# A feed-forward part split into two phases, with both matrix products by Strassen's scheme

## The chip, the core and the metric

The kernel runs on one core of a Trainium2 chip. The metric is the device time of one launch in microseconds (us). TensorE (PE in the profile) multiplies matrices into PSUM, which has eight banks of 128 x 512 floats; VectorE (DVE) and ScalarE (ACT) read and write PSUM and SBUF, GpSimd (POOL) reads and writes SBUF alone, and SyncE (SP) issues the DMAs. Each engine works through its own instructions in order and waits on semaphores.

## The reference

One layer of a streaming encoder trunk is computed for 1024 prompt tokens and 64 sample tokens. The change touches its last lines, the feed-forward part:

```python
D_MODEL = 1024; D_FF = 4 * D_MODEL          # tokens: 1024 + 64
x = x + rms_norm(merged @ lp['w_out'], lp['post_mix_gain'])
u = jax.nn.relu(rms_norm(x, lp['pre_ffn_gain']) @ lp['w_up'])      # 1024 -> 4096
return x + rms_norm((u * u) @ lp['w_down'], lp['post_ffn_gain'])   # 4096 -> 1024
```

## The kernel before

All large products are made in "fp32 parts": an operand x is held as a rounded part hi (ScalarE's copy) and a remainder lo = x - hi (a subtraction on GpSimd or VectorE), both in a type that TensorE takes at full rate, and a product is three matmuls, hi*hi, hi*lo and lo*hi (`three_products`, L315 to L321). The 64 sample tokens are partly multiplied in plain fp32 instead (`product_apart`, L324), in two halves of 64 rows.

`block_out` (L2363) makes the output projection, the residual and the norm, and leaves the normed tokens transposed in f_hi and f_lo (128 x 8 x 1152). It already issues the first four units of the up projection (`up_unit`), and turns the last token group last, so the fifth unit starts at 1569.0 us of the trace.

`block_ffn` (L2587) then goes over eight groups of 512 hidden features. In a group, 12 *up units* (`FF_UPS`: four blocks of 128 features by token groups of 384, 384 and 320) fill a PSUM bank each with 24 matmuls; ScalarE takes relu and square, VectorE the square's remainder, and so u_hi and u_lo for this group stay in SBUF. Then 16 *down units* (two halves of 512 output columns by eight tiles of 128 tokens, 12 matmuls each) and two fp32 products for the sample tokens give partial results, which VectorE adds into the accumulator `big` (L2756). Weights come in four slabs of 1 MB per group through a ring of two places: SP loads, ScalarE rounds (L2695), GpSimd subtracts (L2664). The loop over groups is a hardware loop, and TensorE waits for a slab's split, a bank's release and the squares' remainders. After the last group each tile is squared and summed (ScalarE), multiplied by the gain and given its inverse root (GpSimd), normed and added to x2 (VectorE, `last_norm`), and stored.

Of the kernel before, what the change touches and what calls it, by code (L numbers as in the profile page):

```python
# [126 lines left out]
def build(nc, io):  # L127
    with ExitStack() as ctx:
# [3 lines left out]
        g.sem = lambda name: ctx.enter_context(nc.semaphore(name))  # L132
# [12 lines left out]
        g.d_x2 = dram("d_x2", (T_ALL, D_MODEL))  # L145

# [5 lines left out]
        weight_ring(g)  # L152
        with ExitStack() as first:
# [26 lines left out]
        with ExitStack() as last:  # L180
            g.big = last.enter_context(nc.sbuf_tensor("big", [P, N_TILE * D_MODEL], F32))
# [42 lines left out]
            g.h_at = -(-nc.sbuf_base // 64) * 64  # L224
            g.h_hi = last.enter_context(nc.sbuf_tensor("f_hi", [P, KT, T_PAD], F32R))
            g.h_lo = last.enter_context(nc.sbuf_tensor("f_lo", [P, KT, T_PAD], F32R))
            out = block_out(g)
            ffn = block_ffn(g, out)
            with nc.Block() as block:
                @block.sync  # L230
                def _(sp):
                    out.on_sync(sp)
                    ffn.on_sync(sp)

                @block.tensor
                def _(pe):
                    out.on_tensor(pe)
                    ffn.on_tensor(pe)

                @block.scalar  # L240
                def _(act):
                    out.on_scalar(act)
                    ffn.on_scalar(act)

                @block.gpsimd
                def _(pool):
                    out.on_gpsimd(pool)
                    ffn.on_gpsimd(pool)

                @block.vector  # L250
                def _(dve):
                    out.on_vector(dve)
                    ffn.on_vector(dve)
# [2103 lines left out]
FF_G = 512  # L2357
FK = FF_G // P
FF_UPS = [(f + e, c0, n) for f in range(0, FK, 2) for c0, n in GROUPS for e in range(2)]
# [3 lines left out]
def block_out(g):  # L2363
# [17 lines left out]
    with ExitStack() as ctx:  # L2381
# [22 lines left out]
        stage.up_full, stage.normed = up_full, n2  # L2404
        stage.x2_stored = [(x2_out[j], out_before[j] + 16 * len(range(j, N_TILE, NX))) for j in range(NX)]
# [181 lines left out]
def block_ffn(g, out):  # L2587
    nc, io = g.nc, g.io
    n0 = g.slab
    N_GRP = D_FF // FF_G  # L2590
    g.slab += 4 * N_GRP
    assert n0 % 2 == 0
    w_up, w_down = io["w_up"][0], io["w_down"][0]
    acc = g.big[:].rearrange("p (i c) -> p i c", c=D_MODEL)
    ups = FF_UPS
    downs = [(half, i) for half in range(2) for i in range(N_TILE)]
    NU, ND = len(ups), len(downs)
    B_UP, B_DN = 4, 3
    up_full = out.up_full
    LEAD = 4  # L2600
    with ExitStack() as ctx:
        sb = lambda name, shape, dt=F32: ctx.enter_context(nc.sbuf_tensor("ff_" + name, shape, dt))
        u_hi, u_lo = sb("u_hi", [P, FK, T_PAD], F32R), sb("u_lo", [P, FK, T_PAD], F32R)
        both, u_late = sb("relu_sq", [P, 4, 384]), sb("u_late", [P, FK, DEC])
        relu, sq = both[:, 0:2, :], both[:, 2:4, :]
        ss, expo = sb("ss", [P, N_TILE, 2]), sb("expo", [P, 1])

        x2 = nc.alloc_sbuf_tensor_at("ff_x2", [P, N_TILE, D_MODEL], F32, offset=g.h_at)
        gain = nc.alloc_sbuf_tensor_at("ff_gain", [P, D_MODEL], F32, offset=g.h_at + 4 * N_TILE * D_MODEL)
        junk = both[:].rearrange("p a b -> p (a b)")[:, 0:D_MODEL]  # L2610
        outs = [io["y_prompt"][0, i * P:(i + 1) * P, :] for i in range(TILE_P)] + [io["y_sample"][0]]
        sem = lambda name: g.sem("ff_" + name)
        gain_in, y_squared, roots, normed, y_done, y_out = (sem(n) for n in (
            "gain_in", "y_squared", "roots", "normed", "y_done", "y_out"))
        unfolded, gained = sem("unfolded"), sem("gained")
        (up_free, squared, sq_made, u_ready, dn_full, acc_done) = (sem(n) for n in (
            "up_free", "squared", "sq_made", "u_ready", "dn_full", "acc_done"))

        stage = Stage()
        @stage.sync  # L2620
        def _(sp):
            def load(i, s):

                n, slot = n0 + 4 * i + s, s % 2
                if s < 2:
                    sp.wait_ge(dn_full, i * ND - ND + N_TILE * (s + 1))
                else:
                    sp.wait_ge(g.w_split, n - 1)
                if s < 2:
                    src = w_up[:, bass.ds(i * FF_G + s * 256, 256)].rearrange("(k p) c -> p k c", p=P)  # L2630
                    k = KT
                else:
                    src = w_down[bass.ds(i * FF_G, FF_G), (s - 2) * 512:(s - 1) * 512].rearrange(
                        "(k p) c -> p k c", p=P)
                    k = FK
                sp.dma_start(g.w_raw[:, slot, :].rearrange("p (k c) -> p k c", k=k), src
                             ).then_inc(g.w_loaded[slot], 16)


            with sp.Fori(0, N_GRP - 1) as i:  # L2640
                load(i, 2)
                load(i, 3)
                load(i + 1, 0)
                load(i + 1, 1)
            load(N_GRP - 1, 2)
# [11 lines left out]
        def _(pool):  # L2657
# [10 lines left out]
            with pool.Fori(0, N_GRP - 1) as i:  # L2668
                for s in range(1, 5):
                    split(n0 + 4 * i + s, s % 2)  # L2670
# [200 lines left out]
```

## Time and profile before

| | us |
|---|---|
| median of 3 runs (lowest to highest) | 2325.13 (2324.92 to 2329.96) |
| span of the profiled execution | 2324.8 |
| TensorE busy in the span | 2262.7 (97%) |
| VectorE, ScalarE, GpSimd busy | 1219.2 (52%), 712.7 (31%), 658.6 (28%) |

The profiled execution's own time is its span, 2324.8 us, 0.3 under the median; the trace shows nothing of what lies around it. Busy times of TensorE overlap, as its matmuls are pipelined, so distances between starts are read in place of durations. "Granted clock" is the share of 2.4 GHz that TensorE had.

### The profile page before, as it was taken

To read this page: it belongs to the slowest core of one execution; us is meant where nothing else is said; L and a number is where in the kernel's file an instruction comes from. 1 tells how busy PE (TensorE), PEld (TensorE's weight loads), DVE (VectorE), ACT (ScalarE), POOL (GpSimd) and SP (SyncE) were. 2 spreads that over 40 slices of the span, in tenths; PEclk is the share of its full clock that TensorE was granted. 3 is DMA by queue.
4 is the path that set the end of the run, shared out by engine and by line. 5 is a ranking of instruction groups with operands and counts; after the bars stand their busy time and mean duration, and the time that the engine had idled before them with its cause. 6 is when DMAs were issued, how large, how long until landed. Compare 5 with 4: busy or idle time off the path is not lost. (4 is left out here: it accounts for less than half of the span.)

```text
span 2324.8 us, 40590 instructions
## 1 busy us (share of the span) xinstructions
PE 2262.7 (97%) x16447; PEld 2107.6 (91%) x16447; DVE 1219.2 (52%) x2113; ACT 712.7 (31%) x1483; POOL 658.6 (28%) x742
## 2 busy tenths in 40 slices
PE   7999999999999999999999999999999999999998
PEld 6998999999999889878889999988989889898896
DVE  4125699999992677255543655164323333243335
ACT  5234421212121244455544423252212122121122
POOL 3453631212322788200001221152212112121215
PEclk9999999999999999999999999999999999999999
DMA  5351222323233644532116533140201201112014
GB/s 171 112 139 55 66 85 82 103 81 100 88 101 119 184 137 114 162 111 73 57 45 216 177 122 114 40 145 21 71 19 54 72 18 54 33 40 72 18 54 163
DMA packets 207209, 214.39 MB, mean 92 GB/s; under 512 B 30521, under 2 KB 188433, under 8 KB 207057
## 3 DMA queue, kind: packets, MB, share of 16 engines
q1 hardware_dynamic: 207056, 212.27, 29.1%
q8 instruction: 106, 1.74, 0.3%
q14 instruction: 47, 0.38, 0.1%
HBM read 152.80 MB, written 59.43 MB: 91 GB/s over the span
## 5 line engine op out<-in xcount | busy, mean ns | idle before, releaser
L306 POOL TENSOR_TENSOR w_lo<-w_raw,w_hi 128x2048 fp32r<-128x2048 f32 (+2 forms) x41 | 174.0, 4244 | 593.5 <-ACT w_hi L299 593.5
L2664 POOL TENSOR_TENSOR w_lo<-w_raw,w_hi 128x2048 fp32r<-128x2048 f32 x31 | 143.0, 4613 | 578.6 <-ACT w_hi L2695 578.6
L319 PE MATMUL ps<-f_hi,w_hi 128*128 128x384 f32 (+1 forms) x768 | 251.3, 327 | 1.6 <-ACT ff_relu_sq L2704 1.6
L319 PE MATMUL ps<-h_hi,w_lo 128*128 128x384 f32 (+1 forms) x768 | 250.5, 326 | 0.0
L319 PE MATMUL ps<-h_lo,w_hi 128*128 128x384 f32 (+1 forms) x768 | 250.3, 326 | 0.0
L319 PE MATMUL ps<-f_hi,w_lo 128*128 128x384 f32 (+1 forms) x768 | 250.3, 326 | 0.0
L319 PE MATMUL ps<-h_hi,w_hi 128*128 128x384 f32 (+1 forms) x768 | 250.3, 326 | 0.0
L319 PE MATMUL ps<-f_lo,w_hi 128*128 128x384 f32 (+1 forms) x768 | 250.1, 326 | 0.0
L748 ACT ACTIVATE p_stage<-ps 128x256 f32<-128x256 f32 (+5 forms) x203 | 83.8, 415 | 519.0 <-PE ps L319 519.0
L2756 DVE TENSOR_TENSOR big<-big,ps 128x512 f32<-128x512 f32 x144 | 94.8, 658 | 262.3 <-PE ps L319 244.2
L2743 DVE TENSOR_TENSOR ff_relu_sq<-ff_relu_sq 128x384 f32<-128x384 f32 (+1 forms) x96 | 102.6, 1069 | 208.8 <-ACT ff_relu_sq L2704 208.6
L319 PE MATMUL ps<-w_hi,h_hi 128*128 128x256 f32 x712 | 204.6, 287 | 3.6 <-DVE h_lo L438 3.6
L319 PE MATMUL ps<-w_lo,h_hi 128*128 128x256 f32 x712 | 202.8, 285 | 0.0
L319 PE MATMUL ps<-w_hi,h_lo 128*128 128x256 f32 x712 | 202.7, 285 | 0.0
L319 PE MATMUL ps<-w_hi,ff_u_hi 128*128 128x512 f32 x512 | 200.1, 391 | 0.0
L319 PE MATMUL ps<-w_lo,ff_u_hi 128*128 128x512 f32 x512 | 199.3, 389 | 0.0
L319 PE MATMUL ps<-w_hi,ff_u_lo 128*128 128x512 f32 x512 | 199.2, 389 | 0.0
L1076 DVE MAX8 ix_m<-ix_work 128x8 f32<-128x1024 f32 (+6 forms) x191 | 168.2, 881 | 6.6
L2695 ACT ACTIVATE w_hi<-w_raw 128x2048 fp32r<-128x2048 f32 x31 | 59.2, 1909 | 341.2 <-DMA w_raw<-in_w_up 341.2
L1078 DVE MATCH_REPLACE8 ix_work<-ix_m,ix_work 128x1024 f32<-128x1024 f32 (+6 forms) x184 | 159.0, 864 | 0.0
L319 PEld LDWEIGHTS ps<-f_hi,w_hi 128*128 128x128 f32 x768 | 144.1, 188 | 4.7 <-issue 4.5
L319 PEld LDWEIGHTS ps<-f_lo,w_hi 128*128 128x128 f32 x768 | 144.2, 188 | 0.0
(239 smaller groups left out, 5407.7 us busy)
## 6 DMA issues: line engine op xcount, KB each, us to landing
w_raw<-in_w_in SPq DMA_DIRECT2D x34, 1024.0 KB, 5.5
w_raw<-in_w_up SPq DMA_DIRECT2D x16, 1024.0 KB, 5.6
w_raw<-in_w_down SPq DMA_DIRECT2D x16, 1024.0 KB, 5.2
gm_gate<-d_gate SPq DMA_DIRECT2D x48, 192.0 KB, 2.6
d_gate<-gatef_stage SPq DMA_DIRECT2D x28, 192.0 KB, 2.5
gm_y_raw<-d_y SPq DMA_DIRECT2D x8, 576.0 KB, 5.0
n_x<-in_x_prompt SPq DMA_DIRECT2D x8, 512.0 KB, 9.1
w_raw<-in_w_mem_kv SPq DMA_DIRECT2D x4, 1024.0 KB, 6.3
```

The lines of the kernel that those rows point to most:

```text
L306: engine.tensor_tensor(g.w_lo[:, s, 0:size], g.w_raw[:, s, 0:size], g.w_hi[:, s, 0:size].bitcast(F32), ALU.subtract).then_inc(g.w_split, 1)
L319: last = pe.matmul(out, left(a, kk), right(b, kk), start=(kk == 0 and n == 0), stop=(kk == k - 1 and n == 2))
L748: nc.scalar.activation(stage[0:r, n % NS, 0:c], g.ps[0:r, n % NB, 0:c], sl.func).then_inc(staged, 1)
L1076: link(v.max(m8, sc if it == 0 else left))
L1078: link(v.match_replace(left, m8, sc if it == 0 else left, NEG))
L2664: G.tensor_tensor(g.w_lo[:, slot, :], g.w_raw[:, slot, :], g.w_hi[:, slot, :].bitcast(F32), ALU.subtract).then_inc(g.w_split, 1)
L2695: S.activation(g.w_hi[:, slot, :], g.w_raw[:, slot, :], ACT.Copy).then_inc(g.w_rounded, 1)
L2743: V.tensor_tensor(sq[:, u % 2, 0:n], relu[:, u % 2, 0:n], relu[:, u % 2, 0:n], ALU.mult).then_inc(sq_made, 1)
L2756: V.tensor_tensor(dst, dst, g.ps[:, 4 + d % B_DN, 0:n], ALU.add).then_inc(acc_done, 1)
```

## The change

The feed-forward part becomes two blocks, `block_up` and `block_down`, with all activations u stored to a DRAM tensor d_u (4096 x 1088) between them. Both are products of 2 x 2 blocks and use seven block products in place of eight (Strassen's scheme in Winograd's form), with the sums and differences of blocks made on VectorE.

**Up.** Features go in 16 chunks of 256. The first two are made as before ("plain", eight units beside the four of `block_out`); meanwhile VectorE, GpSimd and ScalarE make the three sums and differences of token blocks (S1, S2, S4, and S3 in the place of a quarter of f_hi and f_lo) with hi and lo parts, each 128 x 2048. The other 14 chunks are seven products of 12 matmuls of 512 columns each. For each chunk four differences of weight blocks (128 x 512) are made on VectorE, seven operands are rounded on ScalarE and subtracted on GpSimd, five PSUM sums (`combine`) and three relu-squares are made on VectorE, and the 64 sample tokens are one fp32 product and one transposition.

**Down.** Four groups of 1024 features. In a group the blocks are 512 tokens by 512 features and 512 features by 512 outputs, seven products of 48 matmuls. Operands have two places each; a product's operands are rounded on ScalarE once the product two before is done, and subtracted on GpSimd (tokens) and VectorE (weights). VectorE makes eight sums of blocks in each group (`make`), keeps 28 PSUM tiles (`keep`), and in the last group GpSimd adds the seven accumulators together (`fold`, five of 128 x 2048, the last two after the operands of products 2 and 3) before the final norm. Two pieces are hung into the last chunk of the up block: the loads of the first two blocks (`early`), and the first weight remainder (`first_lo`), which stands on VectorE ahead of that chunk's last sum.

```diff
-FF_G = 512
-FF_UPS = [(f + e, c0, n) for f in range(0, FK, 2) for c0, n in GROUPS for e in range(2)]
+FF_UPS = [(e, c0, n) for c0, n in GROUPS for e in range(2)]
...
             with nc.Block() as block:
                 def _(sp):
+                    for fresh in up.fresh + down.fresh:
+                        sp.sem_clear(fresh)
                     out.on_sync(sp)
-                    ffn.on_sync(sp)
+                    up.on_sync(sp)
+                    down.on_sync(sp)
...
-def block_ffn(g, out):
+CH, PLAIN = 256, 2
+PARTS = [("11", "X"), ("S1", "Z"), ("S2", "Y"), ("12", "X"), ("S3", "Y"), ("S4", "Z"), ("22", "Y")]
+def block_up(g, out):
...
+    def _(pool):
+        split_slab(g, pool, n0 + 1, SLAB)
+        pool.wait_ge(late_made, 1)
+        G.tensor_tensor(v_c[:], hi.bitcast(F32), low.bitcast(F32), ALU.add).then_inc(raw11, 1)
+        pool.wait_ge(s_hi, 1)
+        G.tensor_tensor(sums["S1"][1][:], v_b[:], sums["S1"][0][:].bitcast(F32), ALU.subtract).then_inc(s_lo_pool, 1)
+        pool.wait_ge(s_hi, 3)
+        G.tensor_tensor(sums["S4"][1][:], v_b[:], sums["S4"][0][:].bitcast(F32), ALU.subtract).then_inc(s_lo_pool, 1)
...
+    def _(act):
+        for u in range(4):
+            relu_plain(u)
+        round_sum(sums["S1"][0][:], v_b[:], 3)
+        relu_plain(4)
+        round_sum(sums["S2"][0][:], v_c[:], 5)
+        relu_plain(5)
+        round_sum(sums["S4"][0][:], v_b[:], 7)
+        hi(PLAIN, 0)
+        relu_plain(6)
...
+    def _(pe):
+        for u in range(UP_EARLY, len(plain)):
+            pe.wait_ge(freed, u - 3)
...
+                if p == 0 and c + 1 < N_CH:
+                    late(c + 1)
+                if p == 3 and c + 1 < N_CH:
+                    turn_late(c + 1)
...
+    def _(dve):
+        square_plain(0)
+        whole(v_a[:], a21)
+        square_plain(1)
+        whole(v_b[:], h_of["22"])
+        square_plain(2)
+        dve.wait_ge(summed, 2)
+        V.tensor_tensor(v_b[:], v_a[:], v_b[:], ALU.add).then_inc(summed, 1)
+        square_plain(3)
+        dve.wait_ge(raw11, 1)
+        V.tensor_tensor(v_a[:], v_c[:], v_a[:], ALU.subtract).then_inc(summed, 1)
+        dve.wait_ge(summed, 3)
+        V.tensor_tensor(v_c[:], v_b[:], v_c[:], ALU.subtract).then_inc(summed, 1)
+        square_plain(4)
+        dve.wait_ge(s_hi, 2)
+        V.tensor_tensor(sums["S2"][1][:], v_c[:], sums["S2"][0][:].bitcast(F32), ALU.subtract).then_inc(s_lo_dve, 1)
+        dve.wait_ge(s_lo_pool, 1)
+        whole(v_b[:], h_of["12"])
+        square_plain(5)
+        dve.wait_ge(summed, 6)
+        V.tensor_tensor(v_b[:], v_b[:], v_c[:], ALU.subtract).then_inc(summed, 1)
+        t_first(PLAIN)
+        square_plain(6)
...
+        square_plain(8)
+        t_second(PLAIN)
...
+        for c in chunks:
+            for j, bank, other, p in ((1, y_bank, v, 4), (2, z_bank, u, 5), (3, y_bank, first, 6)):
+                if j == 3 and c == N_CH - 1:
+                    stage.before_last_sum(dve)
+                combine(made(j), bank, other, [(prod, q_of(c, p) + 1), (combined, n + j + 1)])
+                relu_square(c, j)
...
+def block_down(g, up):
+    def early(sp):
+        load_b(sp, 0, "11")
+        stored(sp, 3)
+        load_a(sp, 0, "11")
...
+    def _(sp):
+        stored(sp, N_CH - 1)
+        sp.wait_ge(up.prod, up.q_of(N_CH - 1, 5) + 1)
+        load_a(sp, 0, "12")
+        load_b(sp, 0, "21")
+        load_b(sp, 0, "12")
+        load_b(sp, 0, "22")
+        sp.dma_start(u_late[:], g.d_u[0:2 * HALF, SEQ:T_ALL].rearrange("(k p) t -> p k t", p=P)).then_inc(l_in, 16)
+        load_a(sp, 0, "21")
+        load_a(sp, 0, "22")
...
+    def _(pool):
+        lo(0, 0)
+        for i in range(N_DG):
+            for p in range(7):
+                if i == LAST and p == 0:
+                    pool.wait_ge(kept, 28 * LAST)
+                    fold(Y2, Z1)
+                    fold(Y1, Z2)
+                if 7 * i + p + 1 < 7 * N_DG:
+                    lo((7 * i + p + 1) // 7, (p + 1) % 7)
+                if i == LAST and p == 0:
+                    pool.wait_ge(kept, 28 * LAST + 4)
+                    pool.wait_ge(folded, 1)
+                    fold(Y2, X1)
...
+    def _(pe):
+            for p, (name, chain) in enumerate(D_PARTS):
+                if p == 2:
+                    late(i, 4 * (chain_no % 2) + 3)
+                pe.wait_ge(a_lo, q + 1)
+                pe.wait_ge(b_lo, q + 1)
...
+        def make(i, j):
+            if j == 0:
+                dve.wait_ge(a_in["21"], 16 * (i + 1))
+                dve.wait_ge(a_in["22"], 16 * (i + 1))
...
+        MAKE_AFTER = {(0, 0): 0, (0, 1): 1, (1, 0): 2, (1, 1): 3, (1, 3): 4, (2, 0): 5, (2, 2): 6, (2, 3): 7}
+        SPLIT_AFTER = {0: 2, 1: 2, 2: 1, 3: 1, 4: 1, 5: 1, 6: 1}
+        normed_at = {(5, 0): 1, (5, 2): 1, (5, 3): 1, (6, 0): 1, (6, 1): 1, (6, 2): 1, (6, 3): 3}
+        for i in range(N_DG):
+            for p in range(7):
+                for t in range(4):
+                    keep(i, p, t)
+                    if (p, t) in MAKE_AFTER:
+                        make(i, MAKE_AFTER[p, t])
+                    if (p, t) == (1, 3):
+                        keep_late(i)
+                    if SPLIT_AFTER[p] == t:
+                        split_next(i, p)
+                    if i < LAST:
+                        continue
+                    if (p, t) == (3, 0):
+                        unfold()
+                    if (p, t) == (5, 0):
+                        dve.wait_ge(gain_in, 16)
+                    for _ in range(normed_at.get((p, t), 0)):
+                        last_norm(n_normed)
+                        n_normed += 1
```

## Rows read from the trace of the kernel before

**Rows 1.** Busy time, share of the span and instructions of each engine.
```profile
PE 2262.7 (97%) x16447; PEld 2107.6 (91%) x16447; DVE 1219.2 (52%) x2113; ACT 712.7 (31%) x1483; POOL 658.6 (28%) x742
```
**Rows 2.** Busy time by stretch (us, engines, clock, DMA): whole feed-forward, one group.
```profile
1569.00:2315.10 746.10, 744.47 (x4002) 666.39 (x4000) 269.88 (x401) 158.99 (x253) 164.08 (x62) 1.00 0.15 52
1623.59:1718.69 95.10, 95.10 (x514) 85.38 (x513) 31.69 (x46) 19.08 (x28) 18.45 (x4) 1.00 0.14 45
```
**Rows 3.** Chain of waits in order of time (start, us, what): one down phase.
```profile
2124.90 69.36 PE ps L319 x384
```
**Rows 4.** Timeline of ACT (start, us): relu at the end of three up units.
```profile
1590.71 0.49 ACT L2704 ACTIVATE ff_relu_sq<-ps 128x384 f32<-128x384 f32 x1 [3.11 <-PE ps L319]
...
1594.87 0.49 ACT L2704 ACTIVATE ff_relu_sq<-ps 128x384 f32<-128x384 f32 x1 [3.11 <-PE ps L319]
...
1598.39 0.44 ACT L2704 ACTIVATE ff_relu_sq<-ps 128x320 f32<-128x320 f32 x1 [2.46 <-PE ps L319]
```
**Rows 5.** Timelines of DVE and POOL: two down units' additions beside a subtraction.
```profile
1604.66 0.69 DVE L2756 TENSOR_TENSOR big<-big,ps 128x512 f32<-128x512 f32 x1 [1.16 <-PE ps L319]
1607.38 0.69 DVE L2756 TENSOR_TENSOR big<-big,ps 128x512 f32<-128x512 f32 x1 [2.03 <-PE ps L319]
...
1604.73 4.61 POOL L2664 TENSOR_TENSOR w_lo<-w_raw,w_hi 128x2048 fp32r<-128x2048 f32 x1 [16.80 <-ACT w_hi L2695]
```
**Rows 6.** Timeline of PE: one fp32 product of the sample tokens, earlier projection.
```profile
158.18 1.97 PE L328 MATMUL ps<-w_raw,h_late 128*64 128x128 f32 x32
```
**Rows 7.** Timelines of DVE and POOL: a square beside a subtraction.
```profile
1583.63 4.71 DVE L2743 TENSOR_TENSOR ff_relu_sq<-ff_relu_sq 128x384 f32<-128x384 f32 x1 [1.19 <-ACT ff_relu_sq L2704]
1588.38 0.56 DVE L2749 TENSOR_TENSOR ff_u_lo<-ff_relu_sq,ff_u_hi 128x384 fp32r<-128x384 f32 x1
...
1583.31 4.62 POOL L2664 TENSOR_TENSOR w_lo<-w_raw,w_hi 128x2048 fp32r<-128x2048 f32 x1 [11.32 <-ACT w_hi L2695]
```
**Rows 8.** Timelines of DVE and POOL: one VectorE product, three GpSimd subtractions in a row.
```profile
1031.96 0.82 DVE L2101 TENSOR_SCALAR at_prob<-at_prob,at_den 128x384 f32<-128x384 f32 x1
...
1030.07 3.84 POOL L1172 TENSOR_TENSOR w_lo<-w_raw,w_hi 128x512 fp32r<-128x512 f32 x3
```
**Rows 9.** Groups of instructions of DVE, by form (busy us, mean ns).
```profile
L306 DVE TENSOR_TENSOR w_lo<-w_raw,w_hi 128x2048 fp32r<-128x2048 f32 x7 | 16.0, 2291 | 61.7 <-ACT w_hi L299 61.7
...
L2764 DVE SCALAR_TENSOR_TENSOR big<-big,ff_ss,ff_gain 128x512 f32<-128x512 f32 x8 | 6.0, 751 | 0.1
```
**Rows 10.** Groups of instructions of POOL, by form, from 1450 us on.
```profile
L2664 POOL TENSOR_TENSOR w_lo<-w_raw,w_hi 128x2048 fp32r<-128x2048 f32 x31 | 143.0, 4613 | 578.6 <-ACT w_hi L2695 578.6
...
L2677 POOL TENSOR_TENSOR big<-big,ff_gain 128x512 f32<-128x512 f32 x8 | 10.2, 1287 | 7.0 <-ACT ff_relu_sq L2726 7.0
...
L2681 POOL TENSOR_TENSOR ff_ss<-ff_ss 128x1 f32<-128x1 f32 x8 | 4.5, 566 | 8.1 <-ACT ff_relu_sq L2726 8.1
```
**Rows 11.** Groups of instructions of ACT, by form, from 1450 us on.
```profile
L2695 ACT ACTIVATE w_hi<-w_raw 128x2048 fp32r<-128x2048 f32 x31 | 59.2, 1909 | 341.2 <-DMA w_raw<-in_w_up 341.2
```
**Rows 12.** Timeline of POOL: the first subtraction of the feed-forward stage.
```profile
1567.36 4.64 POOL L2664 TENSOR_TENSOR w_lo<-w_raw,w_hi 128x2048 fp32r<-128x2048 f32 x1 [13.92 <-ACT w_hi L2695]
```
**Rows 13.** DMA issues by line (KB each, median us to landing).
```profile
w_raw<-in_w_down SPq DMA_DIRECT2D x16, 1024.0 KB, 5.2
...
out_y_prompt<-big SPq DMA_DIRECT2D x8, 512.0 KB, 2.6
```
**Rows 14.** Busy time by stretch: two 1 MB loads at once, ten 256 to 512 KB loads (last: GB/s).
```profile
2271.00:2281.00 10.00, 10.00 (x45) 8.29 (x45) 2.11 (x4) 2.90 (x8) 8.76 (x5) 1.00 1.02 415
1652.00:1657.00 5.00, 5.00 (x31) 5.00 (x30) 0.00 (x0) 1.78 (x1) 0.00 (x0) 1.00 1.04 365
```
**Rows 15.** Who PE waited for (us in total, times, longest).
```profile
PE ps L319 <- DVE f_lo L2563: 3.8, 1, 3.8
...
PE ps L319 <- ACT ff_relu_sq L2704: 1.6, 1, 1.6
```
**Rows 16.** Busy time by stretch, right after the 3.8 us wait (clock third from the end).
```profile
1429.42:1432.83 3.41, 2.88 (x13) 2.91 (x14) 3.41 (x4) 3.41 (x5) 0.00 (x0) 0.50 0.97 284
```

More of the change, by code:

```diff
@@ L247, in _ @@
                     out.on_gpsimd(pool)
-                    ffn.on_gpsimd(pool)
+                    up.on_gpsimd(pool)
+                    down.on_gpsimd(pool)
                 @block.vector
@@ new lines, in block_up @@
+    g.slab += N_CH
+    at = lambda name, shape, offset, dt=F32: nc.alloc_sbuf_tensor_at("up_" + name, shape, dt, offset=offset)
+    KB = 1024
+    q1, q2 = g.big_at, g.rest_at
+    work = [at(f"work{j}", [P, KH, HALF], q1 + 8 * KB * j) for j in range(3)]
+    v_b, v_c, v_a = work
+    sq = at("sq", [P, 4, 384], q1 + 24 * KB)
+    h_late = at("h_late", [P, KT, DEC], q1 + 30 * KB)
+    lt, lu = at("lt", [P, 2, P], q1 + 32 * KB), at("lu", [P, 2, P], q1 + 33 * KB)
+    t3 = at("t3", [P, KH, P], q1 + 34 * KB)
@@ new lines, in block_up @@
+    late_full, late_kept, late_sq, late_turned, late_out = (sem(n) for n in (
+        "late_full", "late_kept", "late_sq", "late_turned", "late_out"))
+    st_out = [sem(f"st_out{j}") for j in range(NST)]
+    lu_out = [sem("lu_out0"), sem("lu_out1")]
+    plain = [(c, e, c0, n) for c in range(PLAIN) for e, c0, n in FF_UPS]
+    q_of = lambda c, p: 7 * (c - PLAIN) + p
+    chunks = range(PLAIN, N_CH)
+    raw = lambda c: g.w_raw[:, c % 2, :].rearrange("p (k f) -> p k f", k=KT)
+    B = lambda c, a, b: raw(c)[:, a * KH:(a + 1) * KH, b * P:(b + 1) * P]
@@ new lines, in block_up, with u_stored @@
+    stage.before_last_store, stage.before_last_sum = None, None
+    stage.last_evicted = [(combined, 5 * len(chunks)), (x_kept, len(chunks)), (late_kept, len(chunks)),
+                          (late_out, len(chunks))]
+    def u_stored(c):
+        counts = [(sq_out[j], 16 * len([u for u in range(len(plain)) if u % 4 == j and plain[u][0] <= c]))
+                  for j in range(4)]
+        made = [out_index(d, j) for d in chunks if d <= c for j in range(4)]
+        counts += [(st_out[j], 16 * len([e for e in made if e % NST == j])) for j in range(NST)]
+        lates = [d for d in chunks if d <= c]
+        counts += [(lu_out[j], 32 * len([d for d in lates if d % 2 == j])) for j in range(2)]
+        return [(s, n) for s, n in counts if n]
```

841 lines of the change are left out of this document (633 added, 208 removed).

## The prediction

> **What bounds the kernel now.** I read the busy line first: TensorE is busy 97% of the span, the others at most half of it [rows 1]. The view by stretch says the same of the feed-forward part alone: from the fifth up unit at 1569.0 to the last product at 2315.1 TensorE works 744.47 of 746.10 us at full clock [rows 2], and the chain of waits runs through whole down phases without another engine in it [rows 3]. So this part is worth its matmuls; what shortens them shortens the kernel as long as the other engines keep up. They have room now: in a group of 95.10 us VectorE has 31.69 and GpSimd 18.45 busy [rows 2].
>
> Prices of matmuls come from distances. A 384-column unit ends 4.16 us after the one before, a 320-column unit 3.52 [rows 4]; a down unit of 12 matmuls of 512 columns takes 2.72 (two additions apart, [rows 5]), or 0.2267 each. A group holds 8 x 4.16 + 4 x 3.52 + 16 x 2.72 = 90.9; the 4.2 left of 95.1 are two fp32 products of the sample tokens, 2.1 each.
>
> The view that matters for the change is the timelines of VectorE and GpSimd laid side by side. A square with both inputs in SBUF that meets a GpSimd subtraction lasts 4.71 us in place of some 0.55 and ends 0.4 after it [rows 7]; the additions with one input in PSUM keep their 0.69 beside the same subtraction [rows 5]. With three subtractions in a row, a VectorE product of SBUF data got in between them (it ended at 1032.78, the run at 1033.91, [rows 8]). I take it that the two engines exclude each other where VectorE reads SBUF alone, and take turns. Before, there are 31 such subtractions, 143 us in all [rows 10], and VectorE's delays land in slack. The change puts far more on both.
>
> **The change, part by part.** *Matmuls, from 1569.0.* Eight plain units: 4 x 4.16 + 4 x 3.52 = 30.7. Up: 14 chunks x 84 x 0.2267 = 266.6. For the sample tokens 14 fp32 products, 1.97 and some 0.1 for the switch, taken as 2.1 [rows 6], and 14 transpositions, no row, bounded by 0.2 and 0.8 (a tenth and two fifths of such a product), taken as 0.4: 35.0. Down: 4 x 28 x 2.72 = 304.6, and four fp32 products of four times the size of those in [rows 2], 4 x 7.1 = 28.4 (bounds 6.8 and 8.4 each). Together 665.3 against 746.1: 80.8 us less.
>
> *Steady chunks, 21.5 us each.* GpSimd has eight operations of 128 x 512 at 1.29 [rows 10] and a small one, about 10.8; VectorE four differences of 0.69, three relu-squares of 0.75 [rows 9], five sums of 0.69, 8.5. The exclusive part is 10.8 + 5.0 = 15.8 of 21.5. The tightest step is the seventh product, which waits for the sum after the fifth; VectorE has it 0.8 after that product ends, 1.9 before it is due. Loads, stores (six small ones a chunk on SP) and rounding (seven of about 0.6 on ScalarE) are a chunk ahead. Cost nothing; cover is the 5.7 us per chunk.
>
> *The plain part.* Here VectorE makes eight sums and remainders of 128 x 2048 (2.29, [rows 9]) until S4 is ready, GpSimd its slab and v_c at 4.6, S1's and S4's remainders and small ones [rows 10], all excluding each other. GpSimd starts at 1567.4 [rows 12]. In turns: slab to 1572.0, square, v_c to 1577.0, then VectorE: sum, square, sum, square, S1 ready 1584.9. ScalarE stands at S1's rounding (1.91, [rows 11]) with the relu of unit 4 behind it: done 1587.4. Unit 8 needs that bank, due 1584.3: 3.2 late. S2 waits for a GpSimd remainder (1587.8 to 1592.4): 1594.7, rounded 1596.6, relu of unit 5 at 1597.1: unit 9, due 1593.7, 3.5 late. S4 (1604.0) holds the relu of unit 6: unit 10, due 1601.4, 5.7 late. Then the relu of unit 9 stands behind the third weight operand, which waits for t_second behind three squares that take turns with GpSimd (1615.6): the first product starts at 1618.5 instead of 1614.6. Sum 16.3.
>
> *Between the phases*, E being the end of the last up product. GpSimd subtracts the first token operand (4.6) from E-5.6, so the first relu-square of the last chunk waits to E-1.0; behind it two sums, two relu-squares and first_lo: the last sum is done at E+4.2, where the down block starts (4.3 lost), the last relu-square at E+5.0, its store lands at about E+7.1 (2.6 for twice the size, [rows 13]). SP waits for that store, and behind it stand six 1 MB loads and the sample tokens' (0.26 MB): 6.55 MB at 365 GB/s [rows 14] are 17.9, and 2.6 before the first byte (5.2 for a lone load [rows 13] less its 2.9): all landed at E+27.7. After the first tile VectorE stands in make 0, which needs the last two of these loads. Behind it: make 1, two keeps, and the weight remainder of product 1, which also lets a token subtraction pass: done E+39.9. Product 1 was due at E+15.2: 24.7 lost. Bounds: 21 (415 GB/s and no subtraction between) and 38 (each load 5.2 after the other).
>
> The Trainium skill, SBUF — State Buffer, section "A bandwidth-pool intuition that's wrong (but worth ruling out)", puts the HBM's side of a core at about 358 GB/s. The loads of rows 14 were above it, at 365 and 415; by the skill's figure the sum would be 0.4 us higher.
>
> *A later down group*, S being its start. GpSimd subtracts to S+6.5, so make 0, asked for at 3.4, ends at 8.8; keep, make 1, keep to 12.5, weight remainder to 14.8. Product 1, due at 10.9, starts 3.9 late. Where the fifth operand meets make 7 in product 3, 1.6 more. Groups 1 and 2: 11.0. The fp32 product (7.1) before product 2 hides the rest.
>
> *The last group* has five folds of 4.6 on GpSimd, two of them ahead of the operand of product 1. Taking turns: fold to 5.3, make 0 to 7.6, fold to 12.2, make 1 to 14.5, operand to 19.1, weight remainder to 21.4: 10.5 late. The next fold and operand go on to 31.3 with makes between: product 2 starts 3.3 late, product 3 2.7, product 4 12.3 (makes 6 and 7, the last fold and two operands are still queued, then unfold and the weight remainder). In product 5 VectorE reaches the first norm at 3.4 but GpSimd has its operand (to 6.5), five gain products of 1.29 and three root steps of about 0.55 [rows 10]: 14.8. The norm takes 2.2, and only then comes the weight remainder of product 6, done at 20.5 against 10.9 due: 9.6 (bounds 6 and 12). Sum 38.4 (bounds 25 and 50).
>
> *The end.* Before, 9.7 from the last product to the end [rows 2]. After, three norms of 2.2 stand on VectorE behind the last tile and then a store: 13.6, 3.9 more.
>
> *Clock.* A 3.8 us wait was followed by 3.41 us at half clock, a loss of 1.7; a 1.6 us wait was not [rows 15, 16]. The waits above make some twelve candidates: 0 to 20; several fall where TensorE waits again anyway, so 8.
>
> SP clears the new semaphores at the block's start, behind no data that is due soon: 0, at most 5.
>
> Sum: -80.8 + 16.3 + 29.0 + 11.0 + 38.4 + 3.9 + 8 = +25.8 on the execution's 2324.8, 2350.6; with the 0.3 to the median, 2351.
>
> **The rivals.**
> *A, the engines pass each other.* If GpSimd's and VectorE's large operations run side by side, and the 4.71 is something of that one line, the plain part loses nothing, the boundary 22 (the loads stay), later groups 0.8 each, the last 3.6 + 9; the clock 6, the end 3.9: -80.8 + 46 = -35, 2290. For it: VectorE's additions pass [rows 5]. Against it: that form reads PSUM, and the delay ends with GpSimd's instruction to 0.4 us [rows 7]. It decides from the point where a remainder of 2.29 stays 2.29 beside a subtraction.
> *B, the waits outside the loads are a third shorter* (55 of 82), because queues slip apart after the first meeting, as each delay of TensorE gives the others time: -80.8 + 55 + 24.7 = -1, 2324. For it: the walk takes every meeting as it comes. Against it: in the plain part and the last group the exclusive work alone (about 48 us from 1567.4, and some 70 in 51 us of products) is more than the time there is.
> *C, the chunks are bound by preparation*: if meetings add 2 us to each of 14 chunks, 2379. For it: seven GpSimd operations a chunk to meet. Against it: the cover of 5.7.
> *D, the products don't shrink*, as a 512-column matmul in the new order takes longer than 0.2267: at 0.24 the 2520 new ones take 34 us more, 2385. Against it: the same form ran at 0.2267 in 16 units of each group.
>
> **How the numbers follow.** The forecast (waits as walked, 2351, own range 2332 to 2375 from the bounds above) gets 0.63; A, and what lies between it and B on the faster side, 0.18; B around no change 0.13; C and D 0.06. A measurement here can't tell a change under 0.3% (7 us) from none. Faster by more 0.19, within 0.13, slower 0.68. The range 2304 to 2376 leaves out the far end of A and C and D.
>
> **What would show it.** In the changed kernel's trace: TensorE from the first Strassen product about 21.5 per chunk without waits; a TensorE wait of 20 to 30 us at the start of the down block, behind VectorE in make 0, which waits for DMA; VectorE remainders of 128 x 2048 with means well over 2.29 beside GpSimd's 4.6; waits before product 1 of each down group, about 4, and 10 in the last; TensorE busy under 95%. I am wrong if VectorE's large operations keep 2.29 in the down phase, if the first loads land before the store of the last chunk, or if chunks take over 23 us.

## The result: 2344 us, 0.8% slower, and the profile after

The changed kernel takes 2344.09 us (2340.34 to 2345.27) where the one before takes 2325.03 beside it: a ratio of 1.0077, 95% interval 1.0063 to 1.0092. The forecast was 2351, slower. The profiled execution spans 2341.4 us against 2324.8, 16.6 more. Of its time 2.1 us lie outside the span; the kernel before, in the executions beside the experiments, has 1.8 there (2325.37 for a span of 2323.6), so the 0.3 that stands ahead of the prediction was too little, by under 2 us.

The busy line of the page: fewer matmuls than in [rows 1] and less TensorE time, GpSimd 205 us busier and VectorE 188.

```profile
PE 2201.6 (94%) x15877; PEld 1999.9 (85%) x15877; DVE 1407.4 (60%) x2093; ACT 761.8 (33%) x1487; POOL 863.2 (37%) x874
```

Busy time by stretch, in the columns of [rows 2] (products are counted from 0 in each group): plain units, the 14 chunks, down group 0, group 1, the last group, and what stands behind the last product.

```profile
1571.00:1617.90 46.90, 38.08 (x234) 36.72 (x233) 42.26 (x22) 11.75 (x19) 26.57 (x9) 0.93 0.18 59
1617.90:1914.05 296.15, 296.15 (x1605) 242.53 (x1603) 140.60 (x164) 84.13 (x152) 149.41 (x124) 1.00 0.31 102
1914.05:2028.05 114.00, 88.04 (x401) 70.66 (x402) 62.00 (x48) 26.25 (x14) 33.67 (x7) 0.88 0.41 141
2028.05:2117.00 88.95, 85.33 (x402) 68.59 (x401) 57.60 (x44) 26.03 (x14) 34.60 (x7) 0.98 0.29 98
...
2206.00:2328.20 122.20, 90.94 (x400) 71.49 (x399) 94.76 (x61) 33.88 (x44) 86.77 (x37) 0.87 0.16 56
2328.20:2341.40 13.20, 0.01 (x1) 0.00 (x0) 9.49 (x15) 1.45 (x4) 6.94 (x11) 0.58 0.54 199
```

The chunks run without a gap, 21.15 us each. All that is lost is lost around them: TensorE's waits from the fifth up unit on (us in total, times, longest) are 73.3 us, where [rows 2] had under 2.

```profile
PE ps L3322 <- issue: 60.8, 8, 22.3
PE ps L336 <- ACT up_sq L2795: 7.0, 2, 5.0
PE ps L3322 <- DVE up_stage_u L2981: 3.7, 1, 3.7
PE ps L2893 <- POOL up_lt L2756: 1.8, 1, 1.8
```

Line 3322 is the down product. "Issue" there means that the view names no releaser; the timelines do. They place the eight waits at product 1 of group 0 (22.3), product 1 of groups 1 and 2 (3.6 each), and products 1, 2, 3, 4 and 6 of the last group (9.9, 1.0, 1.7, 10.7, 8.1).

The longest one, in the chain of waits (start, us, what): the last store of the up phase, SP's seven loads behind it, the preparation (make 0) that needs the last two, its rounding, its remainder, product 1.

```profile
1917.73 0.70 DVE up_stage_u L2985
...
1918.45 2.01 DMA d_u<-up_stage_u
...
1923.02 2.33 SPq L3145
...
1925.39 5.10 SPq L3116
...
1930.53 10.23 DMA dn_a<-d_u
...
1940.86 2.30 DVE dn_at L3408
...
1943.24 1.92 ACT dn_a_hi L3250
...
1945.23 5.09 POOL dn_a_lo L3194
...
1952.57 7.48 PE ps L3322 x20
```

The last two links before product 1 need care. The rounding and GpSimd's remainder are of dn_at, which product 2 reads, and they end 2.2 us before product 1 starts. What product 1 waited for is VectorE's remainder of its weights, which stood behind make 0 and make 1 and then met that GpSimd operation; it ends at 1952.47 (timeline of VectorE).

```profile
1946.47 6.00 DVE L3331 TENSOR_TENSOR dn_b_lo<-dn_b,dn_b_hi 128x2048 fp32r<-128x2048 f32 x1
```

### The profile page after: what moved, and what is told of

It is laid out like the page before. It is cut to its first block and busy times, and to the rows that moved or that the text cites. A ratio compares the mean times of both kernels' runs of the same rounds, so it can differ in the third digit from the quotient of the medians.

```text
span 2341.4 us, 39247 instructions
## 1 busy us (share of the span) xinstructions
PE 2201.6 (94%) x15877; PEld 1999.9 (85%) x15877; DVE 1407.4 (60%) x2093; ACT 761.8 (33%) x1487; POOL 863.2 (37%) x874
## 5 line engine op out<-in xcount | busy, mean ns | idle before, releaser
L3322 PE MATMUL ps<-dn_b_hi,dn_a_hi 128*128 128x512 f32 x448 | 181.6, 405 | 64.5 <-issue 60.8
L3322 PE MATMUL ps<-dn_b_lo,dn_a_hi 128*128 128x512 f32 x448 | 179.6, 401 | 0.0
L3322 PE MATMUL ps<-dn_b_hi,dn_a_lo 128*128 128x512 f32 x448 | 179.2, 400 | 0.0
L336 PEld LDWEIGHTS ps<-h_hi,w_hi 128*128 128x128 f32 x768 | 144.2, 188 | 0.0
L336 PEld LDWEIGHTS ps<-h_hi,w_lo 128*128 128x128 f32 x768 | 144.2, 188 | 0.0
L336 PEld LDWEIGHTS ps<-h_lo,w_hi 128*128 128x128 f32 x768 | 144.2, 188 | 0.0
L336 PEld LDWEIGHTS ps<-w_hi,h_hi 128*128 128x128 f32 x712 | 136.9, 192 | 5.8 <-issue 2.7
L336 PEld LDWEIGHTS ps<-w_lo,h_hi 128*128 128x128 f32 x712 | 137.0, 192 | 0.6
L336 PEld LDWEIGHTS ps<-w_hi,h_lo 128*128 128x128 f32 x712 | 136.9, 192 | 0.0
L336 PE MATMUL ps<-gm_y_hi,w_hi 128*128 128x384 f32 (+1 forms) x384 | 126.6, 330 | 5.7 <-DVE big L2348 4.1
```

What stands on the lines that cost most here:

```text
L336: last = pe.matmul(out, left(a, kk), right(b, kk), start=(kk == 0 and n == 0), stop=(kk == k - 1 and n == 2))
L3322: last = pe.matmul(g.ps[:, bank, :], h[a][:, k, t * P:(t + 1) * P], w[b][:, k, :], start=(chain not in begun and k == 0 and n == 0), stop= ...
```

## The experiments

All are edits of the changed kernel, timed against the kernel before. The last three columns are read from each run's trace: TensorE's waits behind the down phase's first product, the time from that product's start to the last one's end, and what stands behind that. In the listings `relu`, `round`, `hi` are ScalarE's evictions and roundings, `lo` a remainder on GpSimd, `keep` VectorE's eviction of a down tile, `split_next` its remainder of the next product's weights, `unfold` its sums for the sample rows.

| run | us | ratio to before | waits | products | behind |
|---|---|---|---|---|---|
| changed kernel | 2344.09 | 1.0077 [1.0063, 1.0092] | 60.8 | 410.5 | 13.2 |
| the same again | 2343.80 | 1.0063 [1.0039, 1.0088] | 60.6 | 410.8 | 12.6 |
| e1 boundary order | 2334.43 | 1.0032 [1.0017, 1.0048] | 50.2 | 405.3 | 13.1 |
| e7 remainder first | 2336.04 | 1.0039 [1.0025, 1.0053] | 58.8 | 405.1 | 14.2 |
| e2 short token remainder | 2314.56 (one run) | | 34.5 | 380.3 | 13.4 |
| e3 folds on VectorE | 2320.88 | 0.9978 [0.9964, 0.9991] | 33.1 | 377.5 | 26.1 |
| e4 norms later | 2339.93 | 1.0058 [1.0040, 1.0075] | 52.4 | 399.4 | 21.5 |
| e5 relu first | 2344.86 | 1.0075 [1.0054, 1.0095] | 60.4 | 410.5 | 12.5 |
| e5b relu and turn first | 2340.38 | 1.0053 [1.0038, 1.0068] | 60.7 | 409.7 | 14.0 |
| e6 TensorE kept busy | 2345.81 (one run) | | 43.2 | 411.4 | 13.9 |
| all orders, 1 | 2292.15 | 0.9854 [0.9833, 0.9876] | 14.7 | 355.1 | 21.7 |
| all orders, 2 | 2287.45 | 0.9840 [0.9814, 0.9865] | 15.6 | 356.3 | 16.0 |
| all orders, 3 | 2284.66 | 0.9809 [0.9791, 0.9828] | 8.3 | 347.5 | 20.3 |

The control:

> The changed kernel itself, beside the experiments on the same chip: 2340 to 2346, 1.006 to 1.009 of the kernel before. If it is 2338 or less here, part of what the runs with other orders gained is the chip and not the order.

It came out so, with one of four executions at 2336.55: on this chip the gains are the orders'. e5b, e6 and the last two runs with all orders ran on other chips, where the kernel before, timed beside them, took 2327.18 and 2327.08. The intervals of e4 and e5b overlap both of the changed kernel's, so what these two did is read from their traces.

**e2: do VectorE and GpSimd exclude each other?** The walk through the stages rests on it, and rival A denies it.

```
-  G.tensor_tensor(low[:], ra[name][:], hi[:]..., ALU.subtract)
+  ks = slice(0, KH) if q < 2 else slice(0, 1)
+  G.tensor_tensor(low[:, ks], ra[name][:, ks], hi[:, ks]..., ALU.subtract)
```

> GpSimd's token remainder of the down phase is computed for 128x512 of its 128x2048 from the third product on (three quarters of those remainders are left out). My theory: VectorE's 128x2048 operations are held up while GpSimd's run, which makes its weight remainder 3.09 us in the mean against 2.29 alone, and that, with the order on VectorE, is what TensorE waits 3.6 us for in groups 1 and 2. Then the mean falls under 2.5 us and the two waits to 1.5 us or less. The rival, VectorE's order alone (two preparations ahead of the remainder): the mean may fall, and the waits stay at 3 us or more.

VectorE's weight remainders in groups 0 to 2 (busy, mean ns), in the changed kernel:

```profile
L3331 DVE TENSOR_TENSOR dn_b_lo<-dn_b,dn_b_hi 128x2048 fp32r<-128x2048 f32 x18 | 53.0, 2945 | 0.0
```

and in this run:

```profile
L3332 DVE TENSOR_TENSOR dn_b_lo<-dn_b,dn_b_hi 128x2048 fp32r<-128x2048 f32 x19 | 43.9, 2310 | 0.0
```

The mean falls to 2.31, the two waits from 3.6 to 0.5 each, and the down phase is 30.2 us shorter, more than the whole slowdown. VectorE's order was the same, so it is not the cause by itself. In groups 1 and 2 one meeting makes the wait: make 0 of group 1, in the changed kernel and in this run,

```profile
2031.44 5.43 DVE L3408 TENSOR_TENSOR dn_at<-dn_a,dn_a 128x2048 f32<-128x2048 f32 x1
```

```profile
2029.55 2.29 DVE L3409 TENSOR_TENSOR dn_at<-dn_a,dn_a 128x2048 f32<-128x2048 f32 x1
```

is 3.14 shorter, and the wait 3.15. Product 1's weight remainder took 2.28 and 2.29, and its token operand was ready at 2034.73, eight us before product 1 started. In group 0 and the last group a part of the gain may be that GpSimd's own operand is ready sooner; no run parts the two. The Trainium skill, SBUF — State Buffer, section "SBUF: two separate sides", says that a VectorE operation with two SBUF inputs and a GpSimd operation share a pair of ports which one of them holds for its whole instruction; the trace agrees: 2.95 against 2.31.

**e7: the order of one remainder.** In groups 1 to 3:

```
-  keep 0, make 0, keep 1, make 1, keep 2, split_next(i, 0), keep 3
+  keep 0, split_next(i, 0), keep 1, make 0, keep 2, make 1, keep 3
```

> In every later group of the down phase the weight remainder of product 1 goes ahead of the first two preparations, and each of these one eviction later. My theory: it is VectorE's order that makes it late, so the 3.6 us waits of groups 1 and 2 go to 0.5 us or less each, with their half-clock stretches (1.7 us each), and nothing is late behind them: 8 to 11 us less, 2333 to 2336; the last group, where folds come first, gains 0 to 3. The rival, that the preparations then make product 2 late by as much: waits of 2 us or more stand before product 2, and the time stays within 3 us of 2344.

Half hit: 3.6 us before product 1 are gone, and 1.3 and 1.7 stand before products 3 and 4 instead, so the rival's mechanism is there too. The larger part of the gain is the clock's. Group 1 by stretch in this run, granted clock third from the end:

```profile
2028.00:2117.00 89.00, 86.08 (x411) 69.05 (x410) 66.60 (x46) 27.97 (x16) 36.69 (x8) 1.00 0.29 98
```

It was 0.98 above: neither short wait was followed by a half-clock stretch. From the first product to the last, 2.0 us less wait and 8.2 us less of work at half clock (20.8 for 29.0) gave 5.4 us.

**e1: the boundary.** In group 0:

```
-  keep 0, make 0 (waits for the last loads), keep 1, make 1, keep 2, split_next(0, 0), keep 3
+  keep 0, keep 1, keep 2, keep 3, split_next(0, 0), make 0, make 1
```

> In the down phase's first group the weight remainder of product 1 goes ahead of the first two preparations. My theory: the 22.26 us that TensorE waits before product 1 are VectorE's order; the operands of product 1 itself land at 1926.1 and 1928.8 and are rounded by 1930.8, 10 us before the two last token loads are there. Then the wait falls to 3 to 6 us, and because the preparations still wait for the last loads, 3 to 8 us of it come back before product 2: 10 to 16 us less than the changed kernel, 2328 to 2334 us. The rival, that 6.55 MB of loads are the bound of the boundary in any order: the wait before product 1 stays over 15 us, or all of it comes back before product 2, and the time stays within 4 us of 2344.

Timeline of VectorE (start, us): the remainder of product 1 now runs before the last loads are in.

```profile
1929.80 3.54 DVE L3331 TENSOR_TENSOR dn_b_lo<-dn_b,dn_b_hi 128x2048 fp32r<-128x2048 f32 x1
1940.75 2.29 DVE L3408 TENSOR_TENSOR dn_at<-dn_a,dn_a 128x2048 f32<-128x2048 f32 x1 [7.41 <-DMA dn_a<-d_u]
```

The 22.3 us became 4.3 before product 1, and 3.7, 1.6 and 2.3 before products 2 to 4, because the preparations still wait for the loads and then one of them meets GpSimd (make 2 took 6.09): 10.3 us less wait, as my theory had it, and the rival falls. But four waits have more half-clock stretches behind them than one: from product 1 of group 0 through product 1 of group 1 TensorE worked 17.7 us at half clock, against 9.1 (2.7 of the difference stands behind the 3.6 us wait of group 1, which both runs have). The last product came 5.2 us earlier, not 10, and the time is 0.4 over the range.

**e3 and e4: the last group.** e4 moves the normalization alone:

```
-  normed_at = {(5, 0): 1, (5, 2): 1, (5, 3): 1, (6, 0): 1, (6, 1): 1, (6, 2): 1, (6, 3): 3}
+  normed_at = {(5, 3): 3, (6, 0): 1, (6, 1): 1, (6, 2): 1, (6, 3): 3}
```

> The first three row tiles' normalization moves on VectorE from among product 5's evictions of the last group to behind the last of them. My theory: TensorE's 8.07 us before the last product are VectorE waiting 10.59 us for the first root, with the weight remainder of the last product behind it. Then that wait goes to 1 us or less, the work behind the last product grows by no more than 3 us, and the time falls by 5 to 9 us, to 2335 to 2339. The rival, that the remainder would be late anyway because GpSimd's folds hold VectorE up: 4 us or more of the wait stay, and the time is above 2340.

The wait of 8.1 us went to nothing (11.1 us less from the first product to the last, with the half clock), and 8.3 us came back behind the last product, where I expected 3 at most. VectorE's timeline: from the first root on it has nine times three operations and four evictions to do, one after the other.

```profile
2308.55 0.74 DVE L3418 SCALAR_TENSOR_TENSOR dn_late_y<-dn_late_y,dn_ss,dn_gain 64x512 f32<-64x512 f32 x1 [4.53 <-POOL dn_ss L3232]
...
2319.47 0.67 DVE L3360 TENSOR_TENSOR dn_acc<-dn_acc,ps 128x512 f32<-128x512 f32 x1
...
2331.92 0.69 DVE L3425 TENSOR_TENSOR dn_acc<-dn_acc,dn_x2b 128x512 f32<-128x512 f32 x1
```

These 24.1 us, with no gap over 0.5, are the bound; the last product's second tile is evicted at 2319.5, five us after the last tile's product ended. So the stall before the last product and the work behind it are one queue. e3 moves the folds, and the normalization too:

```
-  POOL, last group: fold(Y2, Z1), fold(Y1, Z2) ahead of lo(1); fold(Y2, X1), fold(Y1, X1), fold(Y3, X1) behind lo(1..3)
+  DVE, group before: fold(Y2, Z1) at (3, 3), fold(Y1, Z2) at (4, 3)
+  DVE, last group: fold(Y2, X1) at (4, 2), fold(Y1, X1) at (5, 2), fold(Y3, X1) at (5, 3)
+  normed_at = {(6, 0): 2, (6, 1): 2, (6, 2): 2, (6, 3): 3}
```

> The five sums of whole accumulators go from GpSimd to VectorE and are spread: two into the group before the last (behind products 3 and 4), three into products 4 and 5 of the last; the normalizations stand behind product 5's evictions and the first two of them behind product 6's first. My theory: the last group's 31.3 us of TensorE waits are GpSimd's two sums in a row (11.2 us) ahead of its token remainder, the next sums ahead of later remainders, and the normalization ahead of the weight remainder. Then the waits of the last group fall to 3 to 8 us, the half-clock stretches with them (another 5 to 8 us), the work behind the last product grows by 4 to 9 us because VectorE does the normalizations there: 2312 to 2325. The rival, that GpSimd and VectorE have too much work that can't run at the same time in the last group whoever does the sums: 15 us or more of waits stay, and the time is above 2330.

```profile
2203.00:2292.40 89.40, 85.73 (x402) 68.59 (x400) 63.74 (x51) 33.07 (x42) 44.78 (x17) 0.98 0.16 56
2292.40:2318.50 26.10, 0.00 (x0) 0.00 (x0) 20.33 (x28) 2.17 (x6) 18.56 (x26) 0.59 0.48 171
```

These are the stretches of the last group's products and of what stands behind them. The group now looks like the others: 3.6 us of wait in place of 31.3, with 33 us less from first to last product, and 12.9 given back behind it (4 to 9 expected). This alone brings the kernel 0.2% under the one before, with an interval that just leaves out no change. A fold took 2.49 in the mean on VectorE, 5.82 on GpSimd. The rival, too much exclusive work whoever does it, falls as it was put (15 us of waits, above 2330), though the 12.9 us show that a part of the work only moved.

**e5 and e5b: the plain part.** ScalarE evicts units 4 to 8 ahead of the roundings that wait for VectorE:

```
-  relu 0..3, round S1, relu 4, round S2, relu 5, round S4, hi 0, relu 6, hi 1, relu 7, relu 8, relu_late
+  relu 0..5, round S1, relu 6, round S2, relu 7, hi 0, relu 8, round S4, hi 1, relu_late
```

> In the plain part of the up phase ScalarE evicts units 4 to 8 ahead of the rounding of the sums that they now stand behind, and the first operand of the first chunk is rounded and its remainder made ahead of the last sum. My theory: the 8.8 us of waits there (units 8 and 10, and the turn ahead of the first product) are ScalarE's order, since each waits for an eviction that stood behind a rounding that waits for VectorE. Then 0 to 3 us of wait stay, with no half-clock stretch in them: 6 to 10 us less, 2334 to 2338. The rival, that VectorE and GpSimd bound the plain part (the sums, their remainders and the squares that free the eviction buffers): 6 us or more of wait stay, part of it before the first product, and the time is above 2341.

The units' waits went to nothing, and 12.7 us in place of the 8.8 stood at the next step: a turn of the sample rows that waits for a small square on GpSimd, behind the remainder of S4 and two more (wait, then timeline of GpSimd).

```profile
PE ps L2892 <- POOL up_lt L2756: 12.7, 1, 12.7
```

```profile
1607.37 5.55 POOL L2766 TENSOR_TENSOR up_S_lo<-up_work,up_S_hi 128x2048 fp32r<-128x2048 f32 x1 [6.77 <-ACT up_S_hi L2813]
1612.88 1.57 POOL L2750 TENSOR_TENSOR up_w_lo<-up_t,up_w_hi 128x512 fp32r<-128x512 f32 x1
1614.42 1.50 POOL L2750 TENSOR_TENSOR up_w_lo<-w_raw,up_w_hi 128x512 fp32r<-128x512 f32 x1
1615.89 0.39 POOL L2756 TENSOR_TENSOR up_lt<-up_lt 128x128 f32<-128x128 f32 x1
```

e5b takes that square, and the last evictions, ahead of S4 as well (some squares on VectorE move with them):

```
-  POOL: lo 0, S4 lo, lo 1, lo 2, square_late      ACT: ... relu 8, round S4, hi 1, relu_late, hi 2, relu 9, hi 3, relu 10, 11
+  POOL: lo 0, square_late, lo 1, lo 2, S4 lo      ACT: ... relu 8, relu_late, relu 9, 10, 11, hi 1, round S4, hi 2, hi 3
```

> As the run with evictions first, and the sample rows' square, which TensorE's turn waits for, goes ahead of GpSimd's remainder of the last sum, with the last plain evictions ahead of that sum's rounding. My theory: the 12.7 us that stood before the turn were GpSimd's order (the square stood behind 5.5 us and two chunk remainders), so no more than 3 us stay before the first product and up to 3 before the next two, and of the 8.8 us with 3.4 us of half clock 6 to 9 are gained: 2334 to 2338. The rival, that VectorE's and GpSimd's operations for the sums bound the stage whatever their order: 6 us or more of wait, now before the second to the sixth product of the first chunk, and 2341 or more.

```profile
PE ps L2934 <- ACT up_s L2859: 4.2, 1, 4.2
PE ps L2934 <- DVE up_u L2979: 2.3, 1, 2.3
PE ps L2934 <- ACT up_sq L2796: 1.3, 1, 1.3
```

Now 7.7 us stand before the products of the first chunk, 1.1 less than in the changed kernel, and the time's interval overlaps the control's. The wait is as the rival has it, the time (2340.38) just under its 2341. Two orders failed, so it seems to be the rival: VectorE's and GpSimd's work for the sums bounds this stage, and the order only says where it shows. That is not proved; no run took part of that work away.

**e6: the clock by itself.**

```
+  if (i, p) == (0, 1): 22 x pe.matmul(ps[:, 4], ident, rb["11"][:, 0], start=True, stop=True)
```

> TensorE does 22 fp32 products of 128x512 that nobody reads, in the wait before product 1 of the down phase's first group; nothing else changes. My theory: half the clock's cost is booked in what follows a long wait: in the changed kernel the clock is at half from 3.8 us into the wait to 5.7 us into product 1. With TensorE busy through the wait, product 1 starts where it did (within 1.5 us) and takes 10.9 us in place of 13.7, so everything behind it ends 2.5 to 3 us earlier. The rival, that product 1 is slow for another cause (the loads, VectorE or GpSimd at the same memory): it takes 13 us or more at full clock as well.

The size was wrong: 22 products took 19.1 us, 4.4 were left, and the clock fell in these. So its time decides nothing. Its trace still speaks for the clock: through the 19.1 us the granted clock was 1.00, where in the changed kernel it was at half from 4.1 us into the wait on. And in product 1 matmuls follow each other by 0.43 and, from 1959.1 on, where the granted clock is back, by 0.23; from 1955.0 to 1959.7 no other engine and no DMA is at work, which excludes the rival for these.

```profile
1956.37 0.63 PE L3325 MATMUL ps<-dn_b_lo,dn_a_hi 128*128 128x512 f32 x1
1956.80 0.63 PE L3325 MATMUL ps<-dn_b_hi,dn_a_lo 128*128 128x512 f32 x1
...
1959.48 0.40 PE L3325 MATMUL ps<-dn_b_hi,dn_a_hi 128*128 128x512 f32 x1
1959.71 0.40 PE L3325 MATMUL ps<-dn_b_lo,dn_a_hi 128*128 128x512 f32 x1
```

**All orders together**, in three steps.

```
+  SP: a12, b21, a22 of group 0 loaded behind product 5 of the last chunk, ahead of its last three stores
+  DVE: first_lo one sum earlier; PE: product 0 waits for its own banks only
+  DVE, later groups: make 0 and make 1 in product 6 of the group before; split ahead of makes
+  e3, e5, and squares, gains and first root of the last group from product 4 on
   ... run 2: e5b; make 7 ahead of make 6; unfold in two halves; fold(Y1, X1) at (4, 3)
   ... run 3: make 6 ahead again, make 7 behind split 4; lo 3, lo 4 ahead of S4 lo; gains in product 3
```

> All of the orders together: the plain part's evictions first; loads for the first down group right behind product 5 of the last chunk, token blocks first; the remainder of each product 1 ahead of the preparations, the next group's first two preparations in product 6 of the group before; sums on VectorE as in the run that moves them; squares, gains and the first root of the last group from product 4 on. My theory: TensorE's waits of 64 us in all fall to 5 to 15, the half clock's 18 us to 4 or less, the work behind the last product stays at 13 to 18 us: 2265 to 2290, 0.975 to 0.985 of the kernel before. The rival, that the work that VectorE and GpSimd can't do at the same time bounds the down phase in any order (7 x 4.6 us and 15 x 2.29 us are 66.5 of a group's 79): waits of 2 us and more appear before products 2 to 4 of each group, 25 us or more in all, and the time is above 2300.

> The run with all orders together, with five more: the plain part as in the run beside it; the preparation that the last product needs ahead of the one that the sixth needs, the latter behind the remainder in product 3; the first group's remainder of product 1 one eviction earlier; the sample rows' copies in two pairs; the sum that closes the first half of the top rows in product 4 in place of 5. My theory: of the 25.9 us of TensorE waits there 3 to 8 stay, and the work behind the last product falls from 21.7 to 14 to 18 us, because the roots of the top rows' tiles no longer wait for the sum in product 5: 2255 to 2270, 0.968 to 0.977 of the kernel before. The rival, that the exclusive work of VectorE and GpSimd only moves the waits on: 15 us or more of waits and above 2278.

> The second run with all orders together has 25.8 us of TensorE waits and 16 us behind the last product. Here the first chunk's third and fourth chunk remainders go ahead of the last sum's on GpSimd; the preparation for product 5 is back ahead of the one for product 6, and the latter stands behind product 3's remainder; the four top row tiles' squares and gains fall into product 3 of the last group, where GpSimd was idle for 8 us, and the sample rows' into product 4. My theory: the 8.7 us before the last product there were GpSimd's gains (12.7 us beside VectorE's sums) ahead of its token remainder, so that wait goes to 1 us or less with 5 us of half clock; the first chunk's 6.7 us go to 3 or less; behind the last product stand 9 to 14 us: 2262 to 2273, 0.973 to 0.978 of the kernel before. The rival, that GpSimd and VectorE have no room left beside each other in the last group: 6 us or more before its products 4 to 6, or more than 16 us behind them, and 2280 or more.

They miss their theories' ranges by 2, 17 and 12 us. Run 1 lies between its theory and its rival (14.7 us of waits in the down phase and 11.0 ahead of the first chunk, but under 2300); runs 2 and 3 come out as their rivals say. In run 2 the gains (12.7 us beside VectorE's folds) made the last product 8.7 late; in run 3 that wait is 1.7 and 20.3 us stand behind. The last group's waits and what stands behind it add up to 26.3, 26.8 and 24.8 us in the three runs: what one order takes away before the last product, another puts behind it. That both engines are full there is my reading; no run took work away. In run 3 the waits of TensorE are

```profile
PE ps L3331 <- issue: 8.3, 6, 2.8
PE ps L2936 <- ACT up_s L2861: 5.3, 1, 5.3
PE ps L3331 <- DVE dn_b_lo L3340: 1.9, 1, 1.9
PE ps L2936 <- ACT up_sq L2798: 1.3, 1, 1.3
```

16.8 us in all, 6.6 of them in the first chunk. At 2284.66 it beats both kernels, the one before by 1.9%: with the same products, the order of the work beside them, and which engine makes the folds, decide the sign.

## Why the prediction was right, point by point

| term (us, span) | forecast | measured |
|---|---|---|
| matmuls | -80.8 | -81.0 |
| plain part | 16.3 | 8.8 |
| between the phases | 29.0 | 26.0 |
| down groups 1 and 2 | 11.0 | 7.2 |
| last group | 38.4 | 31.3 |
| end | 3.9 | 3.5 |
| clock | 8 | 17.9 |
| start of the fifth unit | 0 | 2.9 |
| sum | 25.8 | 16.6 |

(Matmuls are what is left: 756.3 from the fifth unit at 1571.9 to 2328.2, less 73.3 of waits and 17.9 of clock, against the 746.1 of [rows 2]. Clock: half of the 35.8 us in which TensorE worked in half-clock stretches. The fifth unit started 2.9 later in this execution, in a part that the change doesn't touch; e1's execution had its first wait 3.0 earlier.)

*The matmuls* were right to 0.2 us in all, where errors cancel: the chunks were 0.35 each under the forecast, the plain part (with the first chunk's sample product) and the down phase over it. Rivals C and D fall: the chunks have no wait, and a 512-column matmul kept its 0.2267.

*Exclusion* was the right cause (e2), and rival A falls: remainders had a mean of 2.95, and make 0 of group 1 took 5.43, as the walk had it (asked for at S+3.4, ended at S+8.8). *Turns* were the step that was mis-sized. The forecast let a waiting GpSimd operation go after the VectorE operation it met. In the plain part VectorE did two sums in a row while S1's remainder stood (timelines of VectorE and GpSimd):

```profile
1587.54 2.28 DVE L3002 TENSOR_TENSOR up_work<-up_work,up_work 128x2048 f32<-128x2048 f32 x1
1589.74 2.28 DVE L3004 TENSOR_TENSOR up_work<-up_work,up_work 128x2048 f32<-128x2048 f32 x1
...
1589.17 7.70 POOL L2763 TENSOR_TENSOR up_S_lo<-up_work,up_S_hi 128x2048 fp32r<-128x2048 f32 x1 [9.51 <-ACT up_S_hi L2812]
```

It took 7.70, of which 4.6 are its own. So S2 was rounded at 1594.0 in place of 1596.6, in an execution that started 2.9 later, and unit 9's 3.5 us were not lost. With that and the smaller delays of the last group (1.0, 1.7 and 10.7 before products 2 to 4 where 3.3, 2.7 and 12.3 were walked) the waits outside the loads were 51 us of the 70 walked, in rival B's direction. But B's 82 count the end and the clock too, and by that count 72 were measured, an eighth less and not a third. Which meetings made the last group's delays smaller is not shown.

*The boundary* went as walked, 22.3 for 24.7: the loads had landed 26.7 us after the last up product (27.7 walked), and make 0 stood 17.9 us for the last two. Of the 22.3 the order in e1 took away 10.3; of the 12.0 that were left, 4.3 stood before product 1, whose remainder came behind the fourth eviction there and met GpSimd (3.54 in place of 2.29), and the rest behind loads and another meeting. With the remainder one eviction earlier and three loads ahead of the last stores, 2.6 and 2.4 were left (runs 2 and 3). So order and loads both count, and no run parts them fully.

*The last group's* five places were as walked, the three large ones nearly in size too (9.9, 10.7 and 8.1 for 10.5, 12.3 and 9.6). e4 shows that the normalization made the last; e3, which moved folds and normalization, leaves the folds for the others.

*The clock* was the other mis-sized term. I took 3.41 us at half clock from [rows 16] for each of some waits; behind long waits TensorE worked up to 5.7 us at half clock, and nine waits had such a stretch, not the four or five that 8 us stand for. The two errors, -21.4 us of waits and +9.9 of clock, partly cancel, and that is luck: with the waits as measured and the clock at the 8 us forecast the sum would have been +6.7, which the prediction itself counts as no change.

## What to carry to other kernels

Before products are traded for sums, add up what VectorE and GpSimd can't do at the same time, stage by stage, and put the operand that TensorE needs next ahead of all preparation on both. When a wait is removed, look for what stood behind it: e5 lost all of its gain at the next step, e4 most of its own behind the last product. And price a wait with the half clock behind it: in e1's first group three of four short waits had such a stretch, 11.6 us of work at half clock against 5.7 behind the one long wait.

## What the runs showed of the hardware that was not expected

VectorE's next operation can go ahead of a GpSimd operation that already waited, even a tiny one. In the last of the runs a sum of 128x1 took 4.12 us while VectorE did six operations from SBUF in a row, and ended when VectorE came to an addition from PSUM at 2258.60 (timeline of GpSimd):

```profile
2250.70 0.38 POOL L3212 TENSOR_TENSOR dn_ss<-dn_ss 128x1 f32<-128x1 f32 x1
...
2253.10 1.54 POOL L3216 TENSOR_TENSOR dn_ss<-dn_ss,dn_expo 128x1 f32<-128x1 f32 x1
2254.61 4.12 POOL L3212 TENSOR_TENSOR dn_ss<-dn_ss 128x1 f32<-128x1 f32 x1
2258.82 0.19 POOL L3214 TENSOR_SCALAR dn_ss<-dn_ss 128x1 f32<-128x1 f32 x1
```

It is no fixed rule: the same sum at 2250.70 took 0.38 while VectorE did operations from SBUF without a gap, so it stood behind one of them at most. No run was made to settle that order. And SP's issue of the sample tokens' load and of the next one took 2.33 and 5.10 us in the chain above, where the four loads before them took 0.37 to 0.70 each.
